# The second layer's modulation products of a two-network kernel, moved out of the first projections

## The reference

```python
for l in range(2):
    mod = silu(c) @ w_ada[l] + b_ada[l]           # image: shift1, scale1, gate1, shift2, scale2, gate2
    mod_c = silu(c_ctx) @ w_ada[l] + b_ada[l]     # the same six for the context
    h = rmsnorm(x) * (1 + scale1) + shift1        # and hc alike
    p = h @ w_in[l]                               # glu, q, k, v and gates
    x = x + gate1 * (merge(p, conv(p), attention(p)) @ w_out[l])
    h2 = rmsnorm(x) * (1 + scale2) + shift2
    x = x + gate2 * (conv_ffn(h2, w_up[l]) @ w_down[l])
```

## Time and profile before

| | |
|---|---|
| time, median of 3 | 2035.17 us (2031.12 to 2044.36) |
| the profiled execution | 2034.59 us |
| its span, first to last instruction | 2032.8 us |
| mean granted TensorE clock | 0.989 |
| busy: PE, PEld, DVE, ACT, POOL | 96%, 82%, 52%, 44%, 58% |
| moved by DMA | 306.57 MB, mean 151 GB/s |
| layer 0's glu to v stages | about 46 to 209 us |
| layer 0's attention, branches and mix | 209 to 451 us |
| norm (0, 2); up; down of layer 0 | 451, 460, 709 to 832 us |
| layer 1 of the first network | 832 to 1302 us |

### The profile page before, as it was taken

The page is one execution under the profiler, slowest core; times in us unless marked ns, Lnnn a source line. Parts: engine busy times, 40 slices in busy tenths (PEclk is TensorE's granted clock), DMA queues, the critical chain, the costliest instruction groups (busy, mean ns, idle before and its releaser), DMA issues.

```text
span 2032.8 us, 34463 instructions
## 1 busy us (share of the span) xinstructions
PE 1953.1 (96%) x12636; PEld 1664.9 (82%) x12636; DVE 1057.8 (52%) x1966; ACT 891.4 (44%) x1513; POOL 1186.9 (58%) x904
## 2 busy tenths in 40 slices
PE   6999999999999999998999999899999999999997
PEld 3766676778888878887889999787899998879997
DVE  2169786626434322688647751885743038565402
ACT  3211444324333332434546654546554354555533
POOL 2333233343445455464586989565588876649895
PEclk8999999999999999999999999999999999999998
DMA  9899231234632333243444567433355564326563
GB/s 390 283 347 340 68 100 56 79 113 81 160 103 83 103 94 93 83 147 103 135 148 141 180 193 227 153 106 95 115 177 178 176 194 149 105 82 181 184 188 102
DMA packets 115688, 306.57 MB, mean 151 GB/s; under 512 B 29673, under 2 KB 44393, under 8 KB 115317
## 3 DMA queue, kind: packets, MB, share of 16 engines
q1 hardware_dynamic: 112664, 298.06, 45.4%
q10 hardware_dynamic: 2908, 6.90, 1.8%
HBM read 300.19 MB, written 8.06 MB: 152 GB/s over the span
## 4 chain that ended last, share of the span: by engine, by line
PE 39%; issue 34%; POOL 21%; DVE 4%; ACT 1%; POOLq 0%; ACTq 0%; DMA 0%; DVEq 0%
POOL w_lo L656 20%; PE bank L1173 11%; PE bank L1175 11%; PE bank L1174 11%; PE bank L1639 1%; PE bank L1640 1%; PE bank L1641 1%; DVE H L1892 1%; DVE rinv L1884 1%; PE bank L1818 1%; DVE u_lo L1892 1%; DVE nb L1884 0%; DVE v_lo L1892 0%; DVE up_g L1892 0%; ACT w_hi L697 0%
## 5 line engine op out<-in xcount | busy, mean ns | idle before, releaser
L656 POOL TENSOR_TENSOR w_lo<-raw,w_hi 128x512 fp32r<-128x512 f32 x884 | 1168.9, 1350 | 824.5 <-ACT w_hi L697 824.0
L697 ACT ACTIVATE w_hi<-raw 128x1024 fp32r<-128x1024 f32 x442 | 466.7, 1057 | 287.8 <-PE bank L1175 231.0
L1173 PE MATMUL bank<-h_hi,w_hi 128*128 128x256 f32 (+1 forms) x1280 | 433.5, 339 | 6.3 <-ACT V L706 2.4
L1175 PE MATMUL bank<-h_hi,w_lo 128*128 128x256 f32 (+1 forms) x1280 | 425.6, 333 | 0.0
L1174 PE MATMUL bank<-h_lo,w_hi 128*128 128x256 f32 (+1 forms) x1280 | 425.6, 332 | 0.0
L1173 PEld LDWEIGHTS bank<-h_hi,w_hi 128*128 128x128 f32 x1280 | 241.0, 188 | 53.8 <-issue 20.5
L1175 PEld LDWEIGHTS bank<-h_hi,w_lo 128*128 128x128 f32 x1280 | 241.1, 188 | 26.4
L1174 PEld LDWEIGHTS bank<-h_lo,w_hi 128*128 128x128 f32 x1280 | 241.2, 188 | 25.4 <-issue 0.2
L1173 PE MATMUL bank<-u_hi,w_hi 128*128 128x272 f32 (+1 forms) x736 | 213.7, 290 | 3.2 <-DVE u_lo L1892 3.2
L1174 PE MATMUL bank<-u_lo,w_hi 128*128 128x272 f32 (+1 forms) x736 | 211.3, 287 | 0.0
L1175 PE MATMUL bank<-u_hi,w_lo 128*128 128x272 f32 (+1 forms) x736 | 211.1, 287 | 0.0
(11 more groups left out here) (341 smaller groups left out, 3688.4 us busy)
## 6 DMA issues: line engine op xcount, KB each, us to landing
raw<-in_wstream SPq DMA_DIRECT2D x442, 512.0 KB, 3.6
ada_raw<-in_wada SPq DMA_DIRECT2D x96, 512.0 KB, 6.4
biash<-rpb_by_offset SPq DMA_DIRECT2D x64, 64.0 KB, 2.9
rpb_by_offset<-in_rpb SPq DMA_DIRECT2D x16, 224.0 KB
bias_by_distance<-vec ACTq DMA_DIRECT2D x1, 3264.0 KB
bias<-bias_by_distance SPq DMA_DIRECT2D x2, 1632.0 KB, 9.0
X<-in_x_in ACTq DMA_DIRECT2D x1, 2048.0 KB, 11.7
bias<-bias_by_distance SPq DMA_DIRECT2D x2, 864.0 KB, 6.1
```

What stands on the lines that cost most here:

```text
L656: i = pool.tensor_tensor(w_lo[:, s, part], raw[:, s, part], w_hi[:, s, part].bitcast(F32), ALU.subtract)
L697: act.activation(w_hi[:, s, :], raw[:, s, :], ACT.Copy).then_inc(sem("w_hi_ready"), 1)
L1173: pe.matmul(o, hi, a_hi, start=start, stop=False)
L1175: return pe.matmul(o, lo, a_hi, start=False, stop=stop)
```

## The change

Units 12 to 23 (groups 3 to 5) leave layer 0's projections. They become 48 pieces of 512 KB in four batches, each loaded ahead to memory that lies idle at the time: "mixed" (group 3, 16 pieces, multiplied in norm (0, 2)), "between" (group 4, 16, norm (1, 1)), "merged" (half of group 5, 8, before layer 1's mix) and "mixed1" (its other half, 8, norm (1, 2)). They take the place of most `keep_busy` matmuls there; the turn of each batch comes a little later. "between" 0 to 4 go to memory that `vec` and `V` use, so SP waits there for `vec_out`.

```diff
+LATE = {"mixed": (3, range(ADA_PIECES), 7), "between": (4, range(ADA_PIECES), 5),
+        "merged": (5, range(0, ADA_PIECES, 2), 5), "mixed1": (5, range(1, ADA_PIECES, 2), 7)}
+LATE_EARLY = 5
...
+            "between": [whole(f"late_b{i}", o) for i, o in enumerate(
+                [q_at + 3 * 4096, V_at, bias_at, cv_at, cv_at + 4096] + [g_at + 4096 * p for p in range(FF_C // 2)])],
+            "merged": [upper(gates, i) for i in range(4)] + [upper(X, 0), upper(X, 1), upper(h_raw, 0), upper(h_raw, 1)],
...
+            def load_late(batch, n):
+                g, pieces, _ = LATE[batch]
+                src = A["wada"][ADA_PIECES * g + pieces[n]].rearrange("p (r t) -> p r t", r=4)
+                sp.dma_start(late_at[batch][n], src).then_inc(sem(f"ada_late_{batch}"), 16)
...
             for u in range(ADA_GROUP + 3, ADA_UNITS):
-                load_ada(u)
+                if u < ADA_FIRST:
+                    load_ada(u)
...
                 if layer == 0:
                     up_slab = gate + 4 * DC
+                    loads(gate + 22)
+                    sp.wait_ge(*after("attn_pv", (0, HEADS // 2 - 1)))
+                    load_late("mixed", 0)
+                    sp.wait_ge(*after("attn_max", (0, HEADS - 1, 1)))
+                    load_late("mixed", 1)
+                    for m in range(DC):
+                        loads(gate + 24 + m)
+                        sp.wait_ge(*after("merged", (0, m)))
+                        load_late("mixed", 2 + m)
+                    sp.wait_ge(*after("chunk", (0, "branch", DC - 1)))
+                    for n in range(2 + DC, ADA_PIECES):
+                        load_late("mixed", n)
                     loads(up_slab + 1)
...
                     for h in range(HEADS):
                         loads(up_slab + 2 + h)
                         spread_rows(1, h)
+                    loads(up_slab + 12)
+                    sp.wait_ge(*after("ada_slab_read", ADA_PIECES * 4 - 1))
+                    sp.wait_ge(*after("vec_out", 0))
+                    for n in range(5):
+                        load_late("between", n)
+                    down_slab = up_slab + 2 * FF_C
+                    for m in range(FF_C // 2):
+                        loads(down_slab + 2 * m + 8)
+                        sp.wait_ge(sem("down_lo"), 2 * m + 2)
+                        load_late("between", 5 + m)
                 else:
+                    loads(gate + 16)
+                    sp.wait_ge(*after("ada_slab_read", ADA_PIECES * 5 - 1))
+                    for n in range(4):
+                        load_late("merged", n)
...
+                    for n in range(2):
+                        load_late("mixed1", n)
+                    loads(gate + 30)
+                    sp.wait_ge(*after("ada_slab_read", (5, 0)))
+                    for n in range(2, 8):
+                        load_late("mixed1", n)
...
+            def late_pieces(batch, lo, hi):
+                g, pieces, b = LATE[batch]
+                if lo == 0:
+                    pe.wait_ge(sem(f"ada_late_{batch}"), 16 * len(pieces))
+                    pe.wait_ge(*after("cs_late", int(batch in ("merged", "mixed1"))))
+                    claim(b)
+                for n in range(lo, hi):
+                    k, half = divmod(pieces[n], 2)
+                    for j in range(2):
+                        q = 32 * (2 * half + j)
+                        mm = pe.matmul(bank[b][q:q + 32, :], cs_late[:, k, :], late_at[batch][n][:, 2 * j:2 * j + 2, :],
+                                       start=k == 0, stop=k == DC - 1, tile_position=(0, q))
...
-                    norm_sum((layer, 1), T_BOTH, False, (0, 6), 11)
+                    norm_sum((layer, 1), T_BOTH, False, late="between")
...
-                    if layer:
+                    u = i + 3
+                    if layer or u > ADA_FIRST:
                         return
...
                     if m == 0:
-                        keep_busy(0, (5, 7)[layer])
+                        if layer:
+                            late_pieces("merged", 0, DC)
+                        else:
+                            keep_busy(0, 5)
                         pe.wait_ge(*after("merge_lo", (layer, DC - 1)))
                     chunk(s, m % 4, T, y_hi, y_lo, (layer, "mix", m), ("mix_out", (layer, m)))
+                    if layer and m == 4:
+                        late_turn(5, "merged", slice(0, 64))
                     s += 1
-                norm_sum((layer, 2), T, False, (7, (4, 6)[layer]), (9, 8)[layer])
+                norm_sum((layer, 2), T, False, late=("mixed", "mixed1")[layer], behind=(0, 4)[layer])
...
                 first_chunks(s, T, h_hi, h_lo, (layer, 2))
+                if layer:
+                    late_turn(6, "mixed1", slice(64, P))
+                else:
+                    late_turn(3, "mixed")
```

More of the change, by code:

```diff
@@ L726, in ada_copy, with late_copy, norm @@
                 copy(ada_part[:, g % 2, :], aux[2 + g % 2][:, :]).then_inc(*done("ada_part_out", g))
+            def late_copy(g, batch, rows=slice(0, P)):
+                act.wait_ge(*after("ada_slab_read", ADA_PIECES * g + ADA_PIECES - 1 if g < 5 else (5, g - 5)))
+                act.wait_ge(*after("ada_turned", g - 1))
+                copy(ada_late[rows, :], bank[LATE[batch][2]][rows, :]).then_inc(*done("ada_part_out", g))
             def root(dst, mean, name, key, m=P):
                 act.activation(dst, mean, ACT.Sqrt, bias=eps[0:m, 0:1]).then_inc(*done(name, key))
-            def norm(tag, X_, T, k_ready, summed=True, slab=None, then=None):
+            def norm(tag, X_, T, k_ready, summed=True, slab=None, then=None, beside=None):
                 for c in range(DC):
@@ L743, in norm @@
                     act.activation(dst, X_[:, c, 0:T], ACT.Square).then_inc(*done("norm_sq", (tag, c)))
+                    if beside is not None and c == 2:
+                        beside()
                 if slab is not None:
@@ L827, in ada_here @@
                 def ada_here(i):
-                    if layer == 0 and i and i % 4 == 0:
+                    if layer == 0 and i in (4, 8):
                         ada_copy(i // 4)
@@ L1243, in keep_busy, with late_turn, norm_sum @@
                     pe.matmul(bank[b][:, 0:2 * P], ident, cst[:, 0:2 * P], start=True, stop=True)
-            def norm_sum(tag, T, summed=True, before=(0, 0), behind=0, reader="norm_root", total=rinv):
+            def late_pieces(batch, lo, hi):
[10 more added lines that the diff above has]
+                                       start=k == 0, stop=k == DC - 1, tile_position=(0, q))
+                    mm.then_inc(*done("ada_slab_read", ADA_PIECES * g + pieces[n]))
+                    if n == len(pieces) - 1:
+                        seen["ada_slab_read", (g, half)] = counts["ada_slab_read"]
+            def late_turn(g, batch, rows=slice(0, P)):
+                b = LATE[batch][2]
+                pe.wait_ge(*after("ada_part_out", g))
+                for j in range(4):
+                    mm = pe.matmul(bank[b][:, 8 * j:8 * j + 8], ada_late[rows, j * P:(j + 1) * P], sel[rows, :], start=True, stop=True)
+                mm.then_inc(*done("ada_turned", g))
+                readers[b] = ("ada_mod", g)
+            def norm_sum(tag, T, summed=True, before=(0, 0), behind=0, reader="norm_root", total=rinv, late=None):
+                if late:
+                    late_pieces(late, 0, LATE_EARLY * len(LATE[late][1]) // ADA_PIECES + 1)
                 if before[1]:
@@ L1951, in ada_mod @@
                 if n == 0:
-                    for st in range(2):
-                        stt(a1[:, layer, :, st], mod[:, layer, DC:2 * DC, st], 1.0, par(layer, "n1g"), ALU.add, ALU.mult)\
-                            .then_inc(*done("scale1_ready", (layer, st)))
+                    scale1(layer)
                 if n == 2:
@@ L1994, in ada_here @@
                 def ada_here(i):
[L1996 removed]
+                    if layer == 0 and i in (6, 10):
                         ada_mod(i // 4)
@@ L2154, in network1 @@
                     if m == 0:
+                        late_vector(layer)
                         dve.wait_ge(*after("gate_out", (layer, 2 * DC - 1)))
@@ L2176, in network1 @@
                         norm_add((layer, 2), m - 1, T)
+                    if layer and m == 5:
+                        late_mod(5, "merged", 4 * DC, DC)
+                        stt(a2[:, 1, :, 0], mod[:, 1, 4 * DC:5 * DC, 0], 1.0, par(1, "n2g"), ALU.add, ALU.mult)\
+                            .then_inc(*done("scale2_ready", 1))
                 norm_add((layer, 2), DC - 1, T)
+                if layer:
+                    dve.wait_ge(*after("scale2_ready", 1))
                 norm((layer, 2), X, T, h_hi, h_lo, scale(a2), shift(3 * DC), parts(layer))
```

78 lines of the change are left out of this document (66 added, 12 removed).

## The result

The changed kernel takes 2068.61 us (median of four runs, 2068.13 to 2074.3), the kernel before 2035.38; the ratio is 1.0164, 95% interval 1.0125 to 1.0202. It is slower by 1.6%, 33 us. I had forecast 2058, so the direction and the mechanism with the largest term hold, and the sum is 11 us short. Its mean granted clock is also the lowest of the four, 0.977 against 0.978 to 0.981, but no trace of the others tells where they gain.

A forecast was written before the change was run, and what follows sets the result against it. PE was busy for 96% of the span, with DVE also at the limit in the q, k and v stages; 2034.6 - 9.2 + 28.4 + 4.0 = 2057.8, so 2058 us, 1.1% slower, range 2045 to 2070.

The forecast's parts named there:

- Part 1: q, k and v stages: some 25 us of work leave PE, DVE limits the gain to -9.2 us, bounds -12 to -5.
- PE now has those scores some 8 us before DVE asks for them: Head 1's scores: DVE loses its 5.56 us wait, part of the 10.3 us by which p_x moves earlier.
- Part 2: Up stage: SP's wait for the distance table delays up 12, PE stands 26.1 us; +28.4 us with low clock, bounds 22 to 36.
- The quick table's rival: Table's DMA from 491 us: an early landing makes SP's wait cost nothing, 2029.4 us; chance 0.06.
- 512.9 us point: Up stage, clock of the kernel before: a table landing before 512.9 us costs PE nothing at up 12.
- Part 3: Pieces, turns and layer 1's delayed loads: +4.0 us together, bounds 0 and 9.
- Ten pieces ahead of the branch slabs ... the ring is nearly as far ahead: +0.4: Layer 1's loads: ten pieces delay them by 13 us, the ring nearly covers it, +0.4 us.
- Before layer 1's mix 8 pieces for 7: +0.7: Before layer 1's mix: 8 pieces at 0.48 us each replace 7 throwaway matmuls of about 0.44 us, +0.7 us.
- dearer everywhere: Rival: clock stays low longer (+6), late pieces or layer 1's loads stall (+5), slow burst (+2): 2071 us; chance 0.13.
- The whole 25 us: Rival, q, k and v stages: DVE isn't the limit, so part 1 would be -25, 2042 us; chance 0.09.
- pieces that aren't ready: Rival: only "between" 15 is close, costing at most 3.6 us of landing, within the range; no chance of its own.

The follow-up runs named there:

- e_units_gone: Kernel before without units 12 to 23 (loads, turns, additions), nothing in their place, layer 1's modulation constant: 2032.32 us, ratio 0.9977 to the kernel before.
- e_v_first: e_wait_later plus ACT copying V ahead of head 0's exponentials in both layers: 2040.71 us, ratio 1.0022 to the kernel before.
- e_wait_later: Changed kernel with SP's wait for the distance table, and the five pieces, ahead of up 20 instead of up 12: 2046.44 us, ratio 1.0051 to the kernel before.
- e_table: Changed kernel with the table's rows first stored to HBM, then copied 128 times from there, copies as slowest dimension: 2044.64 us, ratio 1.0044 to the kernel before.
- e_spread: Changed kernel with layer 1's pieces loaded behind each of several slabs instead of in two lists: 2065.48 us, ratio 1.0139 to the kernel before.
- e_groups: e_wait_later with layer 1's loads spread, X pieces at v 0 and v 1, half batches over four column groups: 2033.67 us, ratio 0.9991.

## Why the prediction was right and wrong

- **Part 1, -9.2 us.** The bound was read rightly: DVE's taps hold PE at 2 us a step, and of 25 us under 5 come out (e_units_gone). The step that failed is "PE now has those scores some 8 us before DVE asks for them". PE didn't have them, because gate 0 stands ahead of them and its bank waits for ACT's copies of V, behind the exponentials, behind DVE's maxima: a wait of 9.0 us that the kernel before, where ACT copies V just as late, hid under the units that were taken out. So p_x came 6.4 us sooner and not 10.3, and behind it 3.0 us were lost again, 2.2 of them by branch 0, with the low clock, where the sum had 1.1. With the copies first (e_v_first) the pause stands where I had it, and the slabs are 7.8 us ahead at up 8. Part 1 was -3.4 in the profiled run and -4 by the medians of e_units_gone, outside my bounds of -12 to -5; of the five traces with this layer 0 only that of e_wait_later, -6.9, is inside. (The work that leaves PE adds up to 25.9 us by the sum's own terms, not 25; nothing hangs on it.)
- **Part 2, +28.4 us.** Right, at +26.4. The pause is 24.3 us against 26.1: the table was seen 9.8 us behind PE's last matmul of up 11, where 11.1 were taken, and PE started 14.5 us behind that, where 15.0 were. By the medians, changed kernel against e_wait_later, part 2 is +23. The wait, the five pieces and the low clock each stand where the text put them. The quick table's rival was real as a mechanism, though not for this kernel: with the copy in another form (e_table) the pause is gone, as its 512.9 us point says, since SP sees the table at 503.8, some 508 in the clock of the kernel before.
- **Part 3, +4.0 us.** This is the term that was mis-sized: +16.7 us in the profiled run, +12.2 in the trace of e_wait_later with the same layer 1 and +14 by the medians, against bounds of 0 to 9. Layer 0 and norm (1, 1) were right (nothing measurable). Two steps failed. "Ten pieces ahead of the branch slabs ... the ring is nearly as far ahead: +0.4": the delay was the forecast's 13 us (SP needed 13.3 for their issue alone), but the ring didn't cover it: branch 0 was late by ACT's 6.64 us, and what was queued behind that rounding (the copies of `pt_x`, then the mean) was not counted; from gate 4 to mix 0 this is 6.5 us over the kernel before, and 0.5 with the loads spread (e_spread). "Before layer 1's mix 8 pieces for 7: +0.7": it was 4 us there (4.1 from mix 0 to mix 4 in the traces of the changed kernel, e_wait_later and e_spread, 0.7 in that of e_groups), because a batch that stays on two column groups runs at half the pace. With the second half batch and the turns behind it, mix 0 to up 10 is 7.5 us over the kernel before, and 2.0 in e_groups. I had taken the price of a piece from the earlier trace rows, where all four groups take turns.
- **The sum.** -9.2 + 28.4 + 4.0 = +23.2 became -3.4 + 26.4 + 16.7 = +39.7 in the profiled run. By the medians it is -4 + 23 + 14 = +33 (e_units_gone for the first, the changed kernel less e_wait_later for the second, the rest for the third). The result lies just inside the range's upper end, 2070, with some luck: two of three parts are outside their bounds, and the profiled run itself, 2074.3, is outside the range. It is nearest to "dearer everywhere", for a reason that this rival named (every new load stands in SP's one queue); the price of two column groups stands in no rival.
- The whole 25 us, and pieces that aren't ready, didn't occur.

What stays open: what sets how long the clock is low in an execution, which goes with 3.5 us between two traces before up 4 alone, and why the old copy is slower than its 12 engines make it.

## What to carry to other kernels

Work that leaves a busy engine takes its cover away with it: before pricing the gain, follow the next thing that engine needs through the other engines' own order of work, here ACT's copies of V. A wait put into the queue that also feeds the weights costs whatever the ring doesn't hold, so put it where its event has passed, and spread extra loads a piece per slab. When moved matmuls use only part of the array, keep the pattern of column groups that their price was read from.

## What the runs showed that I had not expected

- Matmuls of 32 columns that take turns over four column groups come every 0.11 us a record, over two groups every 0.22 us. The Trainium skill's page "TensorE: Matmul & The Clock Gate", Part 3, "Packing small matmuls", says that matmuls at different tile positions run at once in the array; the trace agrees for four groups and shows nothing of it for the two (0 and 32, or 64 and 96) that the half batches used.
- One DMA of 3264 KB took at most 47.6 us from its issue when it read twelve partitions 128 times each, and at most 15.5 us from HBM with the 128 copies as the slowest dimension, ACT's extra wait of 2.7 us beside it.
- SP's issue of a 512 KB load took 0.45 us with 4 KB rows, 0.55 to 0.6 with 1 KB rows alone, and up to 2.2 us on average for two of them behind four others.
